# Sixteen tiles written out in a row, and one loop of 60 rounds with a table for the other tiles of a mixture-of-experts stage

## What is computed

```python
logits = (xf @ w_router + b_router)            # 288 tokens leave the kernel, 32 experts
top_v, top_i = lax.top_k(logits, 4); gates = softmax(top_v)
hmid = x @ w_up[e] + b_up[e]                   # 1024 -> 2048
hg = minimum(hmid[:, :1024], 7.0); hl = clip(hmid[:, 1024:], -7.0, 7.0)
act = hg * sigmoid(1.702 * hg) * (hl + 1.0)
y += gate * (act @ w_down[e] + b_down[e])      # 1024 -> 1024
```

## Time and profile before

| | |
|---|---|
| time, median of 3 runs | 1590.22 us (1586.76 to 1590.52) |
| profiled execution, its own time | 1590.55 us |
| its span | 1588.8 us |
| busy: PE, DVE, POOL, ACT | 87%, 40%, 17%, 13% |
| HBM read | 457.84 MB |
| tiles (from the bias matmul of tile 0 to the end) | 553.6 to 1588.8 us |

### The profile page before, as it was taken

The page is one execution under the profiler, slowest core; times in us unless marked ns, Lnnn a source line. Parts: engine busy times, 40 slices in busy tenths (PEclk is TensorE's granted clock), DMA queues, the critical chain, the costliest instruction groups (busy, mean ns, idle before and its releaser), DMA issues.

```text
span 1588.8 us, 33204 instructions
## 1 busy us (share of the span) xinstructions
PE 1385.0 (87%) x12283; PEld 726.2 (46%) x12284; DVE 638.3 (40%) x1434; ACT 211.6 (13%) x561; POOL 269.0 (17%) x322
## 2 busy tenths in 40 slices
PE   7999999989889999779999988795887987876985
PEld 5778777779776443223333332231332332221332
DVE  3999765544562442214242332141222322212222
ACT  2111332413430210000000000000000000000001
POOL 2008600133310011102121111020111111101100
PEclk9999999999999999889999998897898999988998
DMA  8677676212056699999959999999999898999897
GB/s 190 112 174 133 111 130 128 88 47 61 1 181 227 267 403 418 405 418 415 382 239 381 354 387 420 409 396 419 379 361 388 356 362 357 389 399 415 338 373 291
DMA packets 136125, 464.98 MB, mean 293 GB/s; under 512 B 12334, under 2 KB 67254, under 8 KB 103271
## 3 DMA queue, kind: packets, MB, share of 16 engines
q1 hardware_dynamic: 135839, 463.37, 79.8%
q0 software_dynamic: 48, 0.85, 0.1%
q10 hardware_dynamic: 192, 0.13, 0.0%
HBM read 457.84 MB, written 7.34 MB: 293 GB/s over the span
## 4 chain that ended last, share of the span: by engine, by line
PE 63%; DMA 16%; issue 7%; DVE 6%; SPq 4%; POOL 3%; DVEq 1%; ACT 0%; POOLq 0%
PE psum L1244 18%; DMA arena<-in_w_up 15%; PE psum L1256 9%; PE psum L739 8%; PE psum L1212 5%; PE psum L1230 3%; PE psum L1278 3%; DVE acc L1814 2%; PE psum L1131 2%; PE psum L1221 2%; SPq L443 2%; PE psum L1139 2%; PE psum L822 2%; POOL acc L538 2%; SPq L440 1%
## 5 line engine op out<-in xcount | busy, mean ns | idle before, releaser
L1244 PE MATMUL psum<-arena,gate 128*32 128x512 f32 x3264 | 416.0, 644 | 91.3 <-DMA arena<-in_w_up 91.3
L2352 DVE COPY gate<-psum 128x256 f32<-128x256 f32 x51 | 21.6, 424 | 693.3 <-PE psum L1256 693.3
L739 PE MATMUL psum<-arena 128*128 128x304 f32 (+1 forms) x1024 | 263.9, 420 | 4.0 <-DMA arena<-in_w_in 2.5
L1244 PEld LDWEIGHTS psum<-arena,gate 128*32 128x32 f32 x3264 | 100.3, 114 | 365.4 <-issue 266.0
L739 PEld LDWEIGHTS psum<-arena 128*128 128x128 f32 x1024 | 197.1, 193 | 68.1 <-DMA arena<-in_w_in 3.0
L1256 PE MATMUL psum<-arena,gate 128*32 128x256 f32 x3264 | 188.8, 383 | 2.9 <-DMA arena<-in_w_down 1.8
L662 POOL TENSOR_TENSOR qkv<-qkv 128x192 f32<-128x192 f32 x50 | 80.8, 1616 | 605.9 <-DVE qkv L2303 605.9
L1256 PEld LDWEIGHTS psum<-arena,gate 128*32 128x32 f32 x3264 | 101.1, 110 | 86.9 <-issue 22.4
L1814 DVE SCALAR_TENSOR_TENSOR acc<-arena,pcol,acc x240 | 126.4, 607 | 0.1
L1230 PE MATMUL psum<-qkv 128*128 128x512 f32 x102 | 59.7, 669 | 62.9 <-issue 62.4
L1698 ACT ACTIVATE gate<-psum 128x256 f32<-128x256 f32 x51 | 19.6, 383 | 515.1 <-PE psum L1221 515.1
(11 more groups left out here) (429 smaller groups left out, 1315.4 us busy)
## 6 DMA issues: line engine op xcount, KB each, us to landing
arena<-in_w_up SPq DMA_DIRECT2D x256, 1024.0 KB, 10.8
arena<-in_w_down SPq DMA_DIRECT2D x256, 512.0 KB, 8.2
arena<-in_w_in SPq DMA_DIRECT2D x32, 1024.0 KB, 10.6
arena<-in_w_conf_out SPq DMA_DIRECT2D x4, 1024.0 KB, 5.0
arena<-in_state_dn_S SPq DMA_DIRECT2D x8, 512.0 KB, 7.3
arena<-in_w_dn_out SPq DMA_DIRECT2D x1, 4096.0 KB, 14.9
out_ss<-arena SPq DMA_DIRECT2D x8, 512.0 KB, 6.1
arena<-in_w_out SPq DMA_DIRECT2D x1, 4096.0 KB, 16.7
```

Source lines behind the costliest of these rows:

```text
L739: last = mm(bank[2 * (j % 2) + f][:, 0:cols.stop - cols.start], wring[:, slot, k, P * half:P * (half + 1)], rhs[:, k, cols], start=(k == 0 ...
L1244: last = mm(hidden(q)[v], xgT[:, i, SL * q0:SL * (q0 + 1)], parts(wup[k], q)[v], start=False, stop=(k == KC - 1), skip_group_check=True)
```

## The change

The loop of tiles 2 to 15 becomes 14 bodies written out on GpSimd, TensorE, ScalarE and VectorE. The outer and the inner loop become one loop of SLOTS = 60 rounds. Each round reads a number `nth` from a table of 60 entries (before: 15), and does tile nth + 15 if it is over zero. The body of the tile stands once in it. The order of the tiles and of the skipped rounds stays: a tile in rounds 0, 1, 2 of the first four groups of four, in rounds 0 and 1 of the other eleven. The table is made by other operations on VectorE, at the same place.

```diff
-            with pe.Fori(2, HEAD) as b:
+            for b in range(2, HEAD):
                 tile_step(b)
             nx = pe.value_load(info_i[0:1, 0:1], min_val=0, max_val=XB)
-            with pe.Fori(0, MID) as i:
-                b = pe.value_load(info_i[0:1, bass.ds(i + O_MID, 1)], min_val=0, max_val=XB + MID - 1) + HEAD
-                tile_step(b)
-                with pe.Fori(0, EXTRA) as j:
-                    with pe.If(i + j * MID < nx):
-                        tile_step(b + j + 1)
+            with pe.Fori(0, SLOTS) as m:
+                nth = pe.value_load(info_i[0:1, bass.ds(m + O_MID, 1)], min_val=0, max_val=XB + MID)
+                with pe.If(nth > 0):
+                    b = nth + (HEAD - 1)
+                    tile_step(b)
```

The same edit stands in the programs of GpSimd, ScalarE and VectorE. The table's part:

```diff
-            for j in range(EXTRA):
-                last = v.tensor_scalar(extra[:, :, j], iota_t[0:1, 0:MID], 0.0, None, ALU.mult)
+            for j in range(1 + EXTRA):
+                last = v.tensor_scalar(rank.rearrange("p (i j) -> p i j", i=MID)[:, :, j], iota_t[0:1, 0:MID],
+                                       info[:, 0:1], float(MID * (j - 1)), ALU.subtract, ALU.add)
             then(last)
-            for j in range(EXTRA):
-                last = v.tensor_scalar(extra[:, :, j], extra[:, :, j], info[:, 0:1], -float(MID * j), ALU.add, ALU.add)
-            then(last)
-            then(v.tensor_scalar(extra, extra, 0.0, None, ALU.max))
-            then(v.tensor_tensor(extra, extra, iota_t[0:1, 0:MID].unsqueeze(2).to_broadcast((1, MID, EXTRA)), ALU.min))
-            then(v.tensor_reduce(info[:, O_MID:O_MID + MID].unsqueeze(2), extra, AX.X, ALU.add))
-            then(v.tensor_tensor(info[:, O_MID:O_MID + MID], info[:, O_MID:O_MID + MID], iota_t[0:1, 0:MID], ALU.add))
-            v.tensor_copy(info_i[0:1, O_MID:O_MID + MID], info[:, O_MID:O_MID + MID])
+            then(v.tensor_scalar(rank, rank, 0.0, None, ALU.is_lt))
+            then(v.tensor_tensor_scan(runs, rank, ones[0:1, 0:SLOTS], -1.0, ALU.add, ALU.add))
+            then(v.tensor_tensor(runs, runs, iota_t[0:1, 0:SLOTS], ALU.subtract))
+            then(v.tensor_tensor(info[:, O_MID:O_MID + SLOTS], runs, rank, ALU.mult))
+            v.tensor_copy(info_i[0:1, O_MID:O_MID + SLOTS], info[:, O_MID:O_MID + SLOTS])
```

More of the change, by code:

```diff
@@ L47 @@
 EXTRA = -(-XB // MID)
+SLOTS = MID * (1 + EXTRA)
 O_MID = 1 + NT + NE
@@ L163, in build @@
         iota_e = iota_t[:, 0:NE]
-        info_i = small(O_MID + MID, I32)
+        info_i = small(O_MID + SLOTS, I32)
         brt = small(32)
@@ L275, in build @@
         ixf = temps[:, 2400:2424].rearrange("p (c n) -> p c n", c=3)
-        info = temps[0:1, 2464:2464 + O_MID + MID]
-        extra = temps[0:1, 2464 + O_MID + MID:2464 + O_MID + (1 + EXTRA) * MID].rearrange("p (i j) -> p i j", j=EXTRA)
+        info = temps[0:1, 2464:2464 + O_MID + SLOTS]
+        rank, runs = (temps[0:1, 2464 + O_MID + SLOTS * i:2464 + O_MID + SLOTS * (i + 1)] for i in (1, 2))
         tcmp = zs[:, :, :].rearrange("p k n -> p (k n)")[:, 0:(NT + 1) * NE].rearrange("p (t e) -> p t e", e=NE)
@@ L671, in _ @@
             selected(1)
-            with pool.Fori(2, HEAD) as b:
+            for b in range(2, HEAD):
                 choose(b)
@@ L675, in _ @@
             nx = pool.value_load(info_i[0:1, 0:1], min_val=0, max_val=XB)
[L676 to L683, removed]
+            with pool.Fori(0, SLOTS) as m:
+                nth = pool.value_load(info_i[0:1, bass.ds(m + O_MID, 1)], min_val=0, max_val=XB + MID)
+                with pool.If(nth > 0):
+                    b = nth + (HEAD - 1)
+                    choose(b)
+                    selected(b)
             choose(nx + (NE - 1))
@@ L1727, in _ @@
             copy_choice()
-            with act.Fori(2, HEAD) as b:
+            for b in range(2, HEAD):
                 tile_step(b)
             nx = act.value_load(info_i[0:1, 0:1], min_val=0, max_val=XB)
[L1731 to L1736, removed]
+            with act.Fori(0, SLOTS) as m:
+                nth = act.value_load(info_i[0:1, bass.ds(m + O_MID, 1)], min_val=0, max_val=XB + MID)
+                with act.If(nth > 0):
+                    b = nth + (HEAD - 1)
+                    tile_step(b)
             copy_actt(nx + (NE - 2))
@@ L2388, in _ @@
             place_choice(1)
-            with dve.Fori(2, HEAD) as b:
+            for b in range(2, HEAD):
                 tile_step(b)
             nx = dve.value_load(info_i[0:1, 0:1], min_val=0, max_val=XB)
[L2392 to L2397, removed]
+            with dve.Fori(0, SLOTS) as m:
+                nth = dve.value_load(info_i[0:1, bass.ds(m + O_MID, 1)], min_val=0, max_val=XB + MID)
+                with dve.If(nth > 0):
+                    b = nth + (HEAD - 1)
+                    tile_step(b)
             take_y(nx + (NE - 2))
```

## The result

| | before | changed |
|---|---|---|
| median | 1590.37 us (1586.76 to 1597.21, 4 runs) | 1618.59 us (1614.27 to 1622.32, 4 runs) |
| ratio | | 1.0171, 95% interval 1.0126 to 1.0217 |
| profiled execution, its span | 1590.55, 1588.8 us | 1615.99, 1614.3 us |

In a later measurement the changed kernel was at 1617.73 us against 1590.98 (1.0150, 1.0124 to 1.0177). The change makes the kernel slower by 27 to 28 us; in the two profiled executions by 25.4 us. The forecast was 1610, a loss of 20 us, with a range of 1603 to 1621.

The account below looks back on a forecast made before the run. TensorE's own sequencer work at tile starts was taken as the bound the change touches. Head -5.0, loop passages +22.5, clock +2.4 and table 0 gave +19.9 on the profiled 1590.55: 1610 us, range 1604 to 1621 (1603 to 1621 for 8 in 10).

Parts of the forecast that it names:

- What bounds the kernel: TensorE at tile starts: waits for its own sequencer, 56.0 us in 35 passages of the loop part, show as idle.
- Price of a read and of a skip: Loop passages on TensorE: 0.77 us per table read, 1.45 per skipped round; with the condition, +22.5 us outside weight stalls.
- Stalls take the growth before them: Loop passages ahead of weight stalls: growth of 7.7 us absorbed; issue grows about 30 us, weight waits shrink about 8.
- The clock: TensorE behind long loop passages: all eight outside stalls drop, perhaps tile 19 too, 1.64 us each; +2.4 us (0 to +6).
- The head: Written-out tiles 2 to 15: 11 passages save 0.45 us each, -5.0 us (-2.6 to -5.3), fetching costed at zero.
- Fetch stalls, as a rival: Written-out head: 14 bodies bring 18 instruction packets of 1 us, none hidden, +18 us, 1628; chance 8%.
- The table: VectorE's making of the table, on the way to tile 1: 0 us (bounds -0.3 to +0.5).
- Skips fetch: Rival, skipped rounds in the loop: 1 us of fetch each, some 19 outside stalls, +19 us, 1629; chance 3%.
- The other rivals: In the loop: clock falls after each 1.40 passage, +26 us, 1636, 5%; or weights absorb new idle, 1586, 4%.
- The sums: Loop passages: 19.0 to 26.9 us with both prices at their ends; skips-fetch rival: some 19 of 26 skips outside stalls.

Follow-up runs that it names:

- late reads: TensorE's two register reads per tile moved from tile start to just ahead of their use: kernel before 1549.74 us (0.9727), changed kernel 1572.78 us (0.9874).
- loop of 60 alone: The changed kernel, but with tiles 2 to 15 in a loop again: 1621.00 us against 1590.93 for the kernel before, ratio 1.0196.
- two reads: The changed kernel with the table number read twice in each of the 60 rounds on TensorE: 1660.23 us, ratio 1.0442 to the kernel before.
- head alone: The kernel before with only tiles 2 to 15 written out, its outer and inner loops kept: 1586.23 us against 1590.93, ratio 0.9979.
- written out from 7 on: The kernel before with tiles 2 to 6 in a loop and only 7 to 15 written out: 1588.66 us against 1590.98, ratio 0.9986.

## Why the prediction was right

The mechanism and the sign were right, and the time was in the range, though in its upper part: a loss of 27 to 28 us against the 20 forecast. Step by step:

- *What bounds the kernel.* Right: TensorE's own sequencer at tile starts. Sequencer work at a passage shows as idle, less a lead; the added reads (0.65 us each, one or three) show that the lead doesn't change with what is added, and the late reads show it from the other side, as the same reads behind queued matmuls cost nothing.
- *Price of a read and of a skip.* I took 0.77 for a read, the direct measure is 0.65. The passages were forecast at 1.40, 2.85 and 4.30 and came at 1.38, 2.8 and 4.2. That 1.40 met 1.38 is partly luck: with 0.65 for the read, 1.38 - 0.48 - 0.65 = 0.25 is left for the condition, where I had 0.14. And a skip is (4.19 - 2.80) = 1.39, not 1.45, at the low end of my bounds. Passages outside stalls grew by 21.2 us, not 22.5.
- *Stalls take the growth before them.* Right: issue +28.1 (56.0 to 84.1), waits for weights -9.0 from 845 us on, where I had 30 and 8.
- *The clock.* This is the term that was mis-sized. I expected one or two more drops of the same length, +2.4 us. All eight tiles behind two skips, and tile 19, fell; and the drops were longer. The nine tiles were 20.1 us busier than 15.66 each; before, seven were 11.7. That is +8.4, 6.0 above the forecast and more than the +6 that I had as the upper bound. The profiled 1616.0 is 5.6 above 1610.4. Beside these 6.0, the head gave 1.7 less and the passages cost 1.3 less than forecast; tile 0's later start (+1.3), the shorter end (-1.6) and the parts with stalls (-0.6) were in no term and nearly cancel. The total stayed in the range, with one term outside its bounds, because the others came near their middle.
- *The head.* The passages fell by 0.5, to nothing, a little more than the 0.45 taken. But I cost fetching at zero, with the matmuls as its cover. In tiles 5 and 6 the matmuls don't bound, the loads do, and there the written-out code costs 2 us. Over tiles 0 to 16 the gain was 3.3, not 5.0.
- *Fetch stalls, as a rival.* Wrong as a general stall, right for two tiles. The queue of instructions between 610 and 850 us (packets, MB, share) had 19 packets, none of them in the kernel before, where I had 18 more, and the tiles from 7 on show no idle, 15.59 us from start to start:

```profile
q8 instruction: 19, 0.31, 0.5%
```

- *The table.* VectorE in order of time, the first and the last operation: 2.00 us from start to start, against 2.03 in the earlier trace rows; nothing, as taken.

```profile
562.73 0.64 DVE L2313 TENSOR_SCALAR temps<-misc,temps 1x15 f32<-1x15 f32 x4
...
564.73 0.18 DVE L2322 CAST misc<-temps 1x67 int32<-1x67 f32 x1
```

- *Skips fetch.* No instruction packet from 880 to 1540 us in the changed kernel either. What the Trainium skill, "Runtime: NRT & Kernel Launch", section "Instruction fetch mechanics", says of jumps outside the fetched window didn't come up here.
- *The other rivals.* The clock didn't fall behind passages of 1.3 to 1.5 us outside stalls in any profile. The weights didn't absorb the loop's growth: of the 28.1 us of issue 21.2 are ahead of tiles without a stall.
- *The sums.* Two slips, which don't change the forecast: with both prices at their low ends the passages make 18.5 us, not 19.0; and of the 26 skipped rounds 17 are outside stalls, not 19.

## What to carry to other kernels

Look at the idle time ahead of the first instruction of a loop body, and at what the engine's sequencer does there: a register read from SBUF was 0.65 us and a taken branch 0.2, and here neither was hidden at the body's start, where the queue has run dry. Put such reads behind the first instructions that take long, not ahead of them; that one move was worth more than the whole change lost. When a change adds idle time to TensorE, count the clock with it: behind idle times of 4.2 us TensorE lost 1.4 to 3.0 us more.

## What the hardware showed that was not expected

- TensorE's idle time before a tile and what its clock then did, outside weight stalls. Nearly the same idle time was followed by a drop or by none, so the idle time alone doesn't tell:

| idle, us | dropped | where | lost each, us |
|---|---|---|---|
| 0 to 1.85 | none | all kernels | |
| 1.95 | 1 of 1 | loop of 60 alone, tile 16 | 1.7 |
| 2.0 to 2.1 | 10 of 16 | two reads | 1.7 |
| 2.3 to 2.4 | 2 of 4 | not in before and head alone; in written out from 7 on and two reads | 1.6 |
| 2.65 to 2.8 | 7 of 11 | five of eight with late reads, tile 19 of both changed profiles, not of the loop of 60 alone | 1.4 to 2.9 |
| 3.1 to 3.2 | 19 of 24 | before, head alone, written out from 7 on | 1.6 to 1.7 |
| 4.1 to 4.2 | all 25 | both changed profiles, loop of 60 alone, tile 19 with two reads | 1.4 to 3.0 |
| 6.1 to 6.2 | all 8 | two reads | 1.8 to 2.6 |

- A 16 KB and an 8 KB fetch of instructions, starting 0.8 to 1.5 us apart, came with one piece of weights landing 1.1 to 1.5 us late and all later ones with it, where the loads (1 MB pieces, over 400 GB/s) were the bound. It was so in six profiles of six; that they are the cause is argued from this.
- With the head written out, 182 matmuls and as many weight loads per tile ran without a gap for nine tiles in a row (15.59 us each), so fetching kept up there at about one 16 KB packet per 11 us.
